# Diffusion backbone on one core: the modulation phase with the conditions as stationary operand

## The reference, cut to what matters

```
for l in range(DEPTH):                       # DEPTH = 2
    mod   = jnp.split(jax.nn.silu(c)     @ w_ada[l] + b_ada[l], 6, axis=-1)
    mod_c = jnp.split(jax.nn.silu(c_ctx) @ w_ada[l] + b_ada[l], 6, axis=-1)
    sh1, sc1, g1, sh2, sc2, g2 = (m[:, None, :] for m in mod)
    h = modulate(rmsnorm(x, norm_mix_g[l]), sh1, sc1)     # xn * (1 + scale) + shift
    ...
```

## Time and profile before

| | |
|---|---|
| median of 3 runs | 6993.63 us |
| span of the profiled execution (first to last instruction) | 6989.3 us |
| span of the modulation phase in it | 0 to about 368 us |
| PE busy / DVE busy / ACT busy, share of the whole span | 83% / 41% / 28% |
| granted TensorE clock, mean over the core | 0.915 |
| HBM traffic over the span | 143 GB/s |

### The profile page before, as it was taken

How to read it: one execution, slowest core, us unless ns; L and a number is a source line. 1 busy time by engine, 2 the same in 40 slices (tenths; PEclk the granted TensorE clock), 3 DMA queues, 4 the chain that set the end, 5 groups by cost and what they waited for, 6 DMA issues and landing times. The chain is left out here.

```text
span 6989.3 us, 78523 instructions
## 1 busy us (share of the span) xinstructions
PE 5804.7 (83%) x32272; PEld 4844.7 (69%) x32273; DVE 2834.6 (41%) x2895; ACT 1943.7 (28%) x1888; POOL 262.9 (4%) x304
## 2 busy tenths in 40 slices
PE   8959937569997969946666999989988999989884
PEld 8934415458887745414456899988977999979874
DVE  0020047431112330037526544456476444465575
ACT  0000011121112220011104433345365333354452
POOL 0020001000000020002010000000000000000000
PEclk9979968789999989967778999999999999999997
DMA  6230110321113331010238655567488555576685
GB/s 202 99 114 26 41 32 1 115 77 59 62 59 125 137 136 34 29 40 1 97 139 304 215 179 183 188 205 255 157 293 293 182 176 187 183 253 210 207 288 190
DMA packets 717348, 1008.52 MB, mean 144 GB/s; under 512 B 58801, under 2 KB 571377, under 8 KB 714353
## 3 DMA queue, kind: packets, MB, share of 16 engines
q1 hardware_dynamic: 687184, 927.48, 39.5%
q0 software_dynamic: 13040, 49.29, 1.9%
q10 hardware_dynamic: 16688, 24.91, 1.0%
HBM read 912.73 MB, written 88.87 MB: 143 GB/s over the span
## 5 line engine op out<-in xcount | busy, mean ns | idle before, releaser
L1805 DVE TENSOR_TENSOR moe_wl<-moe_wst,moe_wh 128x2048 fp32r<-128x2048 f32 x630 | 1420.4, 2287 | 691.2 <-ACT moe_wh L1763 689.0
L1691 PE MATMUL ps<-moe_wh,moe_xh 128*128 128x256 f32 x5152 | 1492.0, 290 | 101.4 <-DVE moe_wl L1805 95.6
L1763 ACT CAST moe_wh<-moe_wst 128x2048 fp32r<-128x2048 f32 x630 | 1175.9, 1903 | 1277.4 <-PE ps L1712 1215.7
L1691 PE MATMUL ps<-moe_wl,moe_xh 128*128 128x256 f32 x5152 | 1472.7, 286 | 0.0
L1691 PE MATMUL ps<-moe_wh,moe_xl 128*128 128x256 f32 x5152 | 1472.0, 286 | 0.0
L1691 PEld LDWEIGHTS ps<-moe_wh,moe_xh 128*128 128x128 f32 x5152 | 1004.1, 195 | 113.7 <-DVE moe_wl L1805 99.5
L1691 PEld LDWEIGHTS ps<-moe_wl,moe_xh 128*128 128x128 f32 x5152 | 1004.8, 195 | 7.1
L1691 PEld LDWEIGHTS ps<-moe_wh,moe_xl 128*128 128x128 f32 x5152 | 1003.2, 195 | 0.0
L1712 PE MATMUL ps<-moe_wh,moe_ah 128*128 128x512 f32 x1288 | 416.1, 405 | 162.4 <-DVE moe_al L1810 162.4
L1299 PE MATMUL ps<-hh,up_wh 128*128 128x512 f32 (+1 forms) x1056 | 376.5, 357 | 51.9 <-DVE up_wl L1343 40.0
L1712 PE MATMUL ps<-moe_wl,moe_ah 128*128 128x512 f32 x1288 | 403.3, 394 | 0.0
(11 more groups left out here) (311 smaller groups left out, 6411.7 us busy)
## 6 DMA issues: line engine op xcount, KB each, us to landing
moe_wst<-in_moe_w_gate SPq DMA_DIRECT2D x210, 1024.0 KB, 7.5
moe_wst<-in_moe_w_up SPq DMA_DIRECT2D x210, 1024.0 KB, 10.0
moe_wst<-in_moe_w_down SPq DMA_DIRECT2D x210, 1024.0 KB, 5.0
ada_w<-in_w_ada SPq DMA_DIRECT2D x24, 2048.0 KB, 8.3
down_wst<-in_ffn_w_down SPq DMA_DIRECT2D x66, 512.0 KB, 3.4
proj_w<-in_w_in SPq DMA_DIRECT2D x8, 2048.0 KB, 7.8
four_dft<-in_dft_seq SPq DMA_DIRECT2D x16, 1024.0 KB, 4.5
xs_d<-route_zero SPq DMA_DIRECT2D x1, 16384.0 KB, 53.4
```

The source lines that it names most:

```text
L1691: x = nc.tensor.matmul(ps[:, 2 * kind + p % 2, i * W:(i + 1) * W], xx[:, k, t], w[:, k, :], start=(k == 0 and j == 0), stop=(k == KD - 1 a ...
L1763: nc.scalar.copy(weights(wh, kind, p), weights(wst, kind, p)).then_inc(hi[kind], 1)
L1805: nc.vector.tensor_tensor(weights(wlo, kind, p), weights(wst, kind, p), weights(wh, kind, p).bitcast(F32), ALU.subtract).then_inc(split[ki ...
```

## The change

The roles of the operands are swapped. `act` becomes 128 x 8 x 32, zero except for columns 0 and 1, and is the stationary operand; the weights are the moving operand, 512 columns wide. The array is used as four groups of 32 columns: group j takes k = 4*kk + j for kk = 0 and 1 and writes PSUM partitions 32j to 32j+31, so a chunk takes 8 matmuls of 128 x 32 against 128 x 512 and leaves four partial sums, two rows each, spread over 128 partitions. ACT copies this 128 x 512 bank to `rows` in SBUF. Four small matmuls then take `rows[:, block]` (128 x 128) as stationary operand and a 0/1 table `selq` (128 x 2, ones where partition % 32 is 0 or 1) as the moving one: they add the four partial sums and turn the rows into columns in one step, in the layout of before. These matmuls of chunk i-1 stand on PE behind the matmuls of chunk i.

The host packs `w_ada` into chunks that are contiguous, 16 KB for each partition, and all small vectors into one table `vec` of 128 x 144. SP issues `vec` first, then chunk 0, then `cst` (now 2 columns wider), then the other chunks; a slot is free when `mm_done` has counted its chunk. The loops are written out. GpSimd clears `act`.

```diff
+    RING = 6
+    NCK = 24
-        act = ph.sb("act", [P, KD, 2])
+        vec = ph.sb("vec", [P, NVEC])
+        act = ph.sb("act", [P, KD, 32])
+        rows = ph.sb("rows", [P, 2, 512])
...
             @block.sync
-                    sp.dma_start(S["cst"][:, :], io["cst"]).then_inc(small, 16)
-                    sp.dma_start(cond[:, 0, :], cols(io["c"].rearrange("a d -> (a d)"))).then_inc(small, 16)
...
-                            sp.wait_ge(wfree, i * 6 + (12 * l + s + 1))
-                            sp.dma_start(wring[:, s, :, :], w[:, :, bass.ds(i * 3072 + 512 * s, 512)]).then_inc(wl[s], 16)
+                sp.dma_start(vec[:, :], io["vec"]).then_inc(small, 16)
+                for i in range(NCK):
+                    if i >= RING:
+                        sp.wait_ge(mm_done, i - RING + 1)
+                    sp.dma_start(wring[:, i % RING, :, :].rearrange("p k n -> p (k n)"), io["ada_packed"][i // 12, i % 12]).then_inc(wl[i % RING], 16)
+                    if i == 0:
+                        sp.dma_start(S["cst"][:, :], io["cst"]).then_inc(cst_ld, 16)
...
             @block.tensor
-                                    mm = nc.tensor.matmul(ps[:, s % 2, 2 * m:2 * m + 2], wring[:, s, k, m * P:(m + 1) * P],
-                                                          act[:, k, :], start=(k == 0), stop=(k == KD - 1))
+                def columns(i):
+                    pe.wait_ge(rows_ready, i + 1)
+                    if i >= 2:
+                        pe.wait_ge(evac, i - 1)
+                    for m in range(4):
+                        x = nc.tensor.matmul(ps[:, 4 + i % 2, 2 * m:2 * m + 2], rows[:, i % 2, m * P:(m + 1) * P], sel, start=True, stop=True)
+                    x.then_inc(col_done, 1)
+
+                pe.wait_ge(silu_ready, 1)
+                for i in range(NCK):
+                    pe.wait_ge(wl[i % RING], 16 * (i // RING + 1))
+                    if i >= 2:
+                        pe.wait_ge(rows_ready, i - 1)
+                    for kk in range(2):
+                        for j in range(4):
+                            x = nc.tensor.matmul(ps[32 * j:32 * j + 32, i % 2, :], act[:, 4 * kk + j, :], wring[:, i % RING, 4 * kk + j, :],
+                                                 start=(kk == 0), stop=(kk == 1))
+                    x.then_inc(mm_done, 1)
+                    if i == 0:
+                        pe.wait_ge(cst_ld, 16)
+                    if i >= 1:
+                        columns(i - 1)
+                columns(NCK - 1)
...
             @block.scalar
+                for i in range(NCK):
+                    act_e.wait_ge(mm_done, i + 1)
+                    if i >= 2:
+                        act_e.wait_ge(col_done, i - 1)
+                    nc.scalar.copy(rows[:, i % 2, :], ps[:, i % 2, :]).then_inc(rows_ready, 1)
```

More of the change, by code:

```diff
@@ L50, in _layout @@
                     ("sel8", 8 * P), ("selpair", 4 * P), ("blockg", 2 * P), ("blockm", 130), ("tri", P),
-                    ("pref", NE), ("koff", NE), ("blk", NUNIT), ("half", NUNIT), ("one", 1), ("eps", 1), ("chan", 2 * P), ("row4", 4), ("row2", 2)]:
+                    ("pref", NE), ("koff", NE), ("blk", NUNIT), ("half", NUNIT), ("one", 1), ("eps", 1), ("chan", 2 * P), ("row4", 4), ("row2", 2), ("selq", 2)]:
         CST[name] = (at, n)
@@ L57 @@
 NCST = _layout()
+NVEC = 2 * KD + 96 + 4 * KD
 def constants():
@@ L160, in phase_modulation @@
 def phase_modulation(nc, io, S):
+    RING = 6
+    NCK = 24
     with Phase(nc, "ada") as ph:
-        wring = ph.sb("w", [P, 6, KD, 512])
-        cond = ph.sb("cond", [P, 2, KD])
-        act = ph.sb("act", [P, KD, 2])
[L166 to L171, removed]
+        wring = ph.sb("w", [P, RING, KD, 512])
+        vec = ph.sb("vec", [P, NVEC])
+        act = ph.sb("act", [P, KD, 32])
+        rows = ph.sb("rows", [P, 2, 512])
+        small, cst_ld, zeroed = ph.sem("small_loaded"), ph.sem("constants_loaded"), ph.sem("act_zeroed")
+        wl = [ph.sem(f"w_loaded{s}") for s in range(RING)]
+        silu_ready, mm_done, rows_ready, col_done, evac, mod_done = (
+            ph.sem(n) for n in ("silu_ready", "mm_done", "rows_ready", "columns_done", "evacuated", "mod_done"))
         mod, gmod, ps = S["mod"], S["gmod"], S["ps"]
+        cond = vec[:, 0:2 * KD].rearrange("p (j k) -> p j k", j=2)
+        bias = vec[:, 2 * KD:2 * KD + 96].rearrange("p (l m) -> p l m", l=2)
+        ng = vec[:, 2 * KD + 96:2 * KD + 96 + 4 * KD].rearrange("p (l w k) -> p l w k", l=2, w=2)
+        sel = S["c"]("selq")
         with nc.Block() as block:
@@ L176, in _ @@
             def _(sp):
-                with nc.allow_non_contiguous_dma(reason="vectors as columns"):
-                    sp.dma_start(S["cst"][:, :], io["cst"]).then_inc(small, 16)
-                    sp.dma_start(cond[:, 0, :], cols(io["c"].rearrange("a d -> (a d)"))).then_inc(small, 16)
[L180 to L188, removed]
-                            sp.wait_ge(wfree, i * 6 + (12 * l + s + 1))
-                            sp.dma_start(wring[:, s, :, :], w[:, :, bass.ds(i * 3072 + 512 * s, 512)]).then_inc(wl[s], 16)
+                sp.dma_start(vec[:, :], io["vec"]).then_inc(small, 16)
[5 more added lines that the diff above has]
+                        sp.dma_start(S["cst"][:, :], io["cst"]).then_inc(cst_ld, 16)
@@ new lines, in _ @@
+            @block.gpsimd
+            def _(pool):
+                nc.gpsimd.memset(act[:, :, :], 0.0).then_inc(zeroed, 1)
+            @block.tensor
+            def _(pe):
+                def columns(i):
[20 more added lines that the diff above has]
+                columns(NCK - 1)
@@ L192, in _ @@
             @block.scalar
             def _(act_e):
-                act_e.wait_ge(small, 16 * 9)
+                act_e.wait_ge(small, 16)
+                act_e.wait_ge(zeroed, 1)
                 for j in range(2):
@@ L197, in _ @@
                 a.then_inc(silu_ready, 1)
[L199 to L209, removed]
-                                    mm = nc.tensor.matmul(ps[:, s % 2, 2 * m:2 * m + 2], wring[:, s, k, m * P:(m + 1) * P],
-                                                          act[:, k, :], start=(k == 0), stop=(k == KD - 1))
-                            mm.then_inc(mm_done, 1)
-                            pe.wait_ge(mm_done, i * 6 + (12 * l + s + 1))
-                            pe.sem_inc(wfree, 1)
+                for i in range(NCK):
[3 more added lines that the diff above has]
+                    nc.scalar.copy(rows[:, i % 2, :], ps[:, i % 2, :]).then_inc(rows_ready, 1)
             @block.vector
             def _(dve):
[L218 to L227, removed]
+                dve.wait_ge(small, 16)
+                for i in range(NCK):
+                    l, m = i // 12, 4 * (i % 12)
+                    dve.wait_ge(col_done, i + 1)
+                    nc.vector.tensor_tensor(mod[:, l, m:m + 4, :], ps[:, 4 + i % 2, 0:8].rearrange("p (m j) -> p m j", j=2),
+                                            bc(bias[:, l, m:m + 4], 2), ALU.add).then_inc(evac, 1)
+                dve.wait_ge(evac, NCK)
                 for l in range(2):
@@ L1912, in _ @@
                                                    op0=ALU.mult, op1=ALU.mult).then_inc(od, 1)
-INPUTS = ["x", "c", "ctx", "c_ctx", "w_ada", "b_ada", "norm_mix_g", "norm_ffn_g", "w_in", "w_out", "gla_w_lr", "gla_b_lr",
+INPUTS = ["x", "ctx", "vec", "ada_packed", "w_in", "w_out", "gla_w_lr", "gla_b_lr",
           "gla_norm_g", "mlstm_conv", "mlstm_gate_b", "sgu_w", "sgu_b", "ffn_w_gate", "ffn_w_up", "ffn_w_down", "moe_router",
@@ L1984, in build, with packed_ada, packed_vectors, cols_of @@
         phase_final(nc, io, S, R)
+def packed_ada(w):
+    return np.ascontiguousarray(np.asarray(w).reshape(2, KD, P, 12, 512).transpose(0, 3, 2, 1, 4)).reshape(2, 12, P, KD * 512)
+def packed_vectors(c, c_ctx, b_ada, mix_g, ffn_g):
+    def cols_of(a):
+        return np.asarray(a).reshape(-1, P).T
+    return np.concatenate([cols_of(a) for a in (c, c_ctx, b_ada[0], b_ada[1], mix_g[0], ffn_g[0], mix_g[1], ffn_g[1])], 1)
 def kernel(**inputs):
@@ L1991 @@
     nc = bacc.Bacc("TRN2", target_bir_lowering=False, num_devices=1)
-    shapes = {"cst": constants(), "dft_seq": dft(SEQ), "dft_ctx": dft(CTX)}
+    shapes = {"ada_packed": packed_ada(inputs["w_ada"]),
+              "vec": packed_vectors(*(inputs[n] for n in ("c", "c_ctx", "b_ada", "norm_mix_g", "norm_ffn_g"))),
+              "cst": constants(), "dft_seq": dft(SEQ), "dft_ctx": dft(CTX)}
     arrays, io = {}, {}
```

1 line of the change is left out of this document (added).

## The result

The change takes 6776.7 us (median of 4 runs, 6771.7 to 6780.9), the kernel before 6994.4 us on the same chip (6993.3 to 6996.1): a ratio of 0.969, 95% interval 0.967 to 0.970, or 218 us less. The forecast was 6766 us and 227 us less. The sign, the range and the bound (the transfers) came true; the narrower band in which the forecast itself was put, 6755 to 6772 us, was missed by 5 us. Of two main errors, one made the gain 8 us larger and one made it 15 us smaller, so that the sum came out closer than its parts is luck; the second was of a kind that the prediction did not have.

A forecast was written before the change was run, and what follows sets the result against it. PE's weight loading was taken to bound the modulation phase; with transfers bounding instead, last chunk at 133.6 us plus its tail ends it at 140.8 against 368.1, gaining 227 us: 6766 us, 8-in-10 range 6752 to 6840.

The forecast's parts named there:

- What bounds it before: Modulation phase at the start: PE's loading of 128 x 128 weights sets the pace, 14.11 us from chunk to chunk.
- The clock of L210: Old modulation matmuls: read as running at 1.2 GHz throughout, from 333 ns weight loads, although the stretches say clock 1.00.
- First chunk at 8 to 9 us: Start of the modulation phase: chunk 0, issued second, should land near 8 to 9 us instead of 27.
- Transfer rate, "I take 400 GB/s": Modulation loads: 52.4 MB on one queue at 400 GB/s (ends 387 and 436), 131 us, 5.24 us a chunk.
- In between I take two at once: A chunk's 16 wide records on PE: two column groups overlap, 9 steps of 0.43 us, 3.9 us at clock 1.00.
- the lower end: A chunk's 16 wide records on PE: all four column groups at once, a quarter of 6.9 us, 1.7 us.
- The clock of the forecast (1.00): Modulation matmuls on PE: priced at clock 1.00, 4.8 us a chunk with the selection, under the 5.24 us of the DMA.
- rival 2: Modulation phase: two groups at once but clock 0.50, 9.4 us a chunk, gain 130 us, 6864 us; chance 0.06.
- Rivals 2 and 3: Modulation phase at clock 0.50; rival 3 has groups in turn, 15.4 us a chunk, 7005 to 7013 us, chance 0.07.
- Hidden: Modulation phase: ACT's copy, 0.585 us a chunk, DVE's add, 0.17 us, constants' wait and GpSimd's clearing cost nothing extra.
- rival 1: Modulation phase: groups don't run side by side, PE bounds at 7.8 us a chunk, 6825 or 6832 us; chance 0.22.
- Everything behind them as long as before: Phases behind `gmod`: unchanged in length, with 2 us allowed for the next phase's clock; more than a few us means wrong.

The follow-up runs named there:

- before's compute with the new loads: Kernel before with PE, ACT and DVE programs kept, but the change's SP program, packed chunks and `vec`; 6974.7 us, ratio 0.997.
- unpacked run: The change with chunks read from `w_ada` itself in 2 KB pieces instead of packed; 6788.7 us, ratio 0.971.
- 117 increments: The change with 117 increments of an unused semaphore at the head of PE's program; 6755.9 us, ratio 0.966.
- the repeat: The change itself run once more, unaltered, beside the padded kernels on the same chip; 6776.3 us, ratio 0.969.

## Why the prediction held, and where it did not

- **What bounds it before** held. The account of the 235.5 us uses the 14.11 us a chunk that the prediction read from the earlier trace rows, and before's compute with the new loads kept it.
- **The clock of L210**, read as 0.50 from the 333 ns loads although its stretch said 1.00: consistent with what the change shows, where the selection's 128 x 128 loads take 338 ns while its eight matmuls take 1.87 us, and 192 when they take 1.05. The granted clock of the first stretches is no reading in the change either: the row of 2 to 10 us says 1.00, and the chunk that starts at 9.25 takes 3.64 us.
- **First chunk at 8 to 9 us**: 9.25.
- **Transfer rate, "I take 400 GB/s"**: 428 to 430. The term was mis-sized: the two single microseconds with `cst` in them (436, 468) were nearer than the long stretch with 2 KB pieces (387). The unpacked run has 386 and confirms that it is the length of the pieces. Its effect: 140.8 forecast for the phase's end, 132.6 measured; 5.8 of the 8 us are the last chunk's matmuls, which start at 127.8 instead of 133.6. The Trainium skill, "DMA: Bandwidth & Descriptors", Specifications, gives 435 GB/s as the ceiling of the path to SBUF; the 430 here lie just below it.
- **"In between I take two at once"**, 9 steps of 0.43 us, 3.9 us: wrong. The step that failed is "if records start in program order, the second record of group j runs beside the first of group j+1". Records of different groups start within 0.02 us of each other at 1.00; the 16 take 1.92 us, four at once, which was the lower end. It changed the pace by nothing, since both lie under the transfers, and the end by the 2 us that the last chunk's matmuls are shorter. The Trainium skill, "TensorE: Matmul & The Clock Gate", Part 3, has three column tiles run 2.38 times as fast as in turn. No run here has three; with two and four groups the steps of 0.43 us give factors of 2 and 4, the full number of groups, and the whole of the 16 records 1.94 and 3.67 (7.05 us over 3.63 and 1.92). Of strictly ordered ends the modelled ends can say nothing.
- **The clock of the forecast (1.00)** was half right: 0.76 over 10 to 100 us, chunks at either level. It cost little, since a chunk at 0.50 takes 5.5 us with four at once, where rival 2 had priced 9.4 with two. Rivals 2 and 3 supposed 0.50 throughout, and no run of the swapped form had that: with two groups PE was granted 0.98 over the same stretch, with one 1.00. The sign that the prediction gave for them, selection loads of 333 ns, did show (up to 338), but in some chunks only.
- **Hidden**: copy, add, constants and clearing held. Chunk 1 starts at 18.82 against 18.3 worked out in rival 1.
- **Rival 1** had the right price for what it supposed: 199.5 to 206.5 us, measured 204.2 when one group was run. Emptying PE: last wide start to first selection start is some 0.55 us there (50.03 less 43.04 and 15 x 0.43), 0.12 more than the pace, near the 0.16 us that the prediction took. The Trainium skill, "TensorEngine Tiling (Array Packing)", Key Properties, has a change of tiling drain the engine. The 0.12 us allow it, but no run separates them from another cause.
- **"Everything behind them as long as before"**, which rested on "behind this phase every engine has the same instructions": the step that failed, and the prediction had named it among its signs of being wrong. The same instructions took 14.9 us longer, since their places in PE's program had moved. That the same instructions take the same time was taken for granted; the earlier trace rows could not show it, and the 2 us allowed for the next phase's clock (1.2 measured) was the only doubt. With the program placed as by 117 increments, the change gives 238 us.

The misses add up: 8 us more gain at the front, 1 and 15 us less behind it, so the spans differ by 219 us where 227 were forecast.

## What to carry to other kernels

A product with two rows belongs with the few rows as the stationary operand: a narrow moving operand pays the loading of weights for every 128 columns (216 ns a record here, at the half clock), and column groups then let the array take 512 columns of four k at once; two groups were enough, since 2 MB came only every 4.9 us. Once transfers are the bound, look at pieces and queue order: long rows gave 428 against 386 GB/s, and one wide table in place of eight loads of single numbers, with `cst` behind the first chunk, started the work 18 us earlier. In a program of tens of thousands of instructions, any edit that changes an engine's count ahead of a dense phase should be timed at several placements before its last 1 to 2% are believed: here 101 or 117 idle increments made the best version, 6756 us, 20 us below the change and 238 below the kernel before.

## What was not expected of the hardware

- The place of a dense loop's instructions costs up to 137 us of 3164, in waits of up to 3.6 us with no semaphore behind them, at fixed matmuls of the loop, only in the passes that jump over the longer version of each step, and, where they are longer than 1 us, always behind a 16 KB packet of the instruction queue. 53 and 181 extra instructions cost 112 and 100 us of the median, 101 and 117 save 20, 245 cost 7 (with `gmod` 6.6 us later, as the increments hold PE until 38.9 us). Why certain places are so bad is open.
- Matmuls of different column groups do not queue behind each other even within a pair of records of one f32 matmul: 1.92, 3.63 and 7.05 us for the same 16 records with four, two and one groups.
- With four groups PE was granted 0.76 on average over 10 to 100 us, busy 69 of 90 us (0.80 and 66 in the repeat); with two it was granted 0.98, busy 81 us, and with one 1.00, busy all 90. The same work in half the steps ran at the lower clock, and cost nothing only because transfers hid it. What decides it no run here shows.
